# Expert products chunk by chunk for all token groups, with the down products one expert behind

## The reference

```python
logits = (x @ w_router) + b_router
top_v, top_e = lax.top_k(logits, 4)              # 4 of 32 experts per token
gates = jax.nn.softmax(top_v, axis=-1)
gu = xe @ w_gu[e] + b_gu[e]                      # xe: the rows routed to expert e, 1024 wide
gate = jnp.minimum(gu[:, :1024], 7.0)
up = jnp.clip(gu[:, 1024:], -7.0, 7.0)
act = (up + 1.0) * gate * jax.nn.sigmoid(1.702 * gate)
y = act @ w_down[e] + b_down[e]                  # weighted by the gate and added per token
```

## Time and profile before

| | us |
|---|---|
| median of 3 runs | 1584.15 |
| span of the profiled execution | 1586.3 |
| PE busy | 1548.4 (98%) |
| VectorE busy | 792.2 (50%) |
| ScalarE busy | 277.8 |
| Pool busy | 187.4 |
| gate-up products (L1333, both tiles) | 691.0 |
| down products (L1339 and L1345) | 343.3 |

### The profile page before, as it was taken

One profiled execution on the slowest core, in us unless ns is written; L12 is line 12 of the kernel. 1 busy time (PEld: TensorE's weight loads), 2 busy tenths in 40 slices (PEclk: granted clock), 3 DMA queues, 4 the chain that ended last, 5 costly groups with the idle time before them and its releaser, 6 DMA issues.

```text
span 1586.3 us, 32991 instructions
## 1 busy us (share of the span) xinstructions
PE 1548.4 (98%) x13237; PEld 717.9 (45%) x13237; DVE 792.2 (50%) x2047; ACT 277.8 (18%) x554; POOL 187.4 (12%) x269
## 2 busy tenths in 40 slices
PE   9999999999999999999999999999999999999995
PEld 7677487787745633333333333333333333333331
DVE  4349738605533645444544454445444544454448
ACT  2310020005311112111111121111111111111113
POOL 3634310014200000000000000000000000000000
PEclk9999999999999899999999999999999999999998
DMA  6555755723160599999999999999999999999995
GB/s 240 160 167 187 260 170 174 253 68 125 65 279 27 193 384 417 413 417 410 415 414 416 410 415 415 413 406 416 414 413 403 419 415 415 405 417 415 413 392 199
DMA packets 72618, 509.62 MB, mean 321 GB/s; under 512 B 13482, under 2 KB 13930, under 8 KB 47330
## 3 DMA queue, kind: packets, MB, share of 16 engines
q1 hardware_dynamic: 62298, 489.15, 77.3%
q0 software_dynamic: 10256, 19.61, 3.7%
HBM read 497.51 MB, written 19.88 MB: 326 GB/s over the span
## 4 chain that ended last, share of the span: by engine, by line
PE 70%; DMA 24%; DVE 2%; issue 1%; ACT 1%; POOL 1%; SPq 0%; DVEq 0%; POOLq 0%; ACTq 0%
PE PS L1333 33%; DMA weight_ring<-w_gu 22%; PE PS L938 16%; PE PS L1246 4%; PE PS L1339 3%; PE PS L989 2%; PE PS L1054 2%; PE PS L1345 2%; PE PS L1040 1%; PE PS L1104 1%; PE PS L1003 1%; DVE weight_ring L1844 1%; DMA y_k<-region_x,idx_y 1%; POOL weight_ring L632 1%; PE PS L1290 1%
## 5 line engine op out<-in xcount | busy, mean ns | idle before, releaser
L1333 PE MATMUL PS<-weight_ring,region_experts 128*32 128x512 f32 x5376 | 599.4, 594 | 8.5 <-DMA weight_ring<-w_gu 6.9
L1333 PEld LDWEIGHTS PS<-weight_ring,region_experts 128*32 128x32 f32 x5376 | 170.1, 110 | 404.0 <-issue 365.4
L1778 DVE TENSOR_TENSOR region_experts<-PS,region_w 128x512 f32<-128x512 f32 x96 | 66.4, 692 | 457.2 <-PE PS L1333 457.1
L1339 PE MATMUL PS<-weight_ring,act_turned 128*32 128x512 f32 x2048 | 225.6, 592 | 0.0
L938 PE MATMUL PS<-region_x,region_w 128*128 128x260 f32 (+1 forms) x928 | 209.4, 385 | 1.0 <-DVE region_x L1560 1.0
L938 PEld LDWEIGHTS PS<-region_x,region_w 128*128 128x128 f32 x928 | 175.2, 190 | 33.1 <-issue 4.6
L1769 DVE STREAM_TRANSPOSE region_experts<-region_x 32x256 f32<-32x256 f32 x372 | 161.2, 433 | 4.7
L865 ACT ACTIVATE region_experts<-region_experts 128x256 f32<-128x256 f32 x96 | 40.0, 417 | 627.4 <-DVE region_experts L1780 627.4
L1339 PEld LDWEIGHTS PS<-weight_ring,act_turned 128*32 128x32 f32 x2048 | 66.6, 110 | 153.2 <-issue 153.2
L1345 PE MATMUL PS<-weight_ring,act_turned 128*32 128x256 f32 x2048 | 117.7, 382 | 4.0 <-DVE act_turned L1790 4.0
L670 POOL DMA_INDIRECT y_k<-region_x,idx_y x32 | 30.1, 940 | 677.9 <-ACT region_x L888 580.7
(11 more groups left out here) (282 smaller groups left out, 1131.8 us busy)
## 6 DMA issues: line engine op xcount, KB each, us to landing
weight_ring<-w_gu SPq DMA_DIRECT2D x112, 2048.0 KB, 12.0
weight_ring<-w_down SPq DMA_DIRECT2D x64, 2048.0 KB, 12.4
ring_more<-w_gu SPq DMA_DIRECT2D x16, 2048.0 KB, 21.6
region_w<-w_mt SPq DMA_DIRECT2D x33, 512.0 KB, 3.9
weight_ring<-cache_kT SPq DMA_DIRECT2D x64, 256.0 KB, 4.0
weight_ring<-cache_v SPq DMA_DIRECT2D x64, 256.0 KB, 3.9
weight_ring<-w_out SPq DMA_DIRECT2D x2, 2048.0 KB, 10.1
weight_ring<-y_k SPq DMA_DIRECT2D x2, 2048.0 KB, 13.2
```

The costliest lines, as they stand in the source:

```text
L1333: mm = pe.matmul(bank(g)[GRP * q:GRP * q + GRP], hTe[u][:, k, GRP * g:GRP * g + GRP], weights(k // 2, u)[:, k % 2, SEG * q:SEG * q + SEG], ...
L1339: mm = pe.matmul(bank(3)[GRP * j:GRP * j + GRP], actT[:, kk, GRP * g:GRP * g + GRP], w_dn[:, kk, 512 * h:512 * h + 512], start=(kk == 0), ...
L1778: dve.tensor_tensor(gu, bank(g), b_wide, ALU.add).then_inc(S["biased"], 1)
```

## The change

PE now computes gate-up products chunk by chunk, all three groups within a chunk, so a chunk is given free when the third group has used it (`up`). The down products of an expert (`down`) come behind the gate-up products of the next one. There are two `actT` for that, and the down products go by halves: wide and rest products of a half together, then the half is free. The comparison and the indices are made for the expert after the next. VectorE's work of an expert is one `step`: wait for the gathered rows of the next expert and turn them, spread this expert's bias, spread the gates, `keep`, compare for the expert after the next, the three groups one after the other, and the indices of the expert after the next; Pool then gathers for these. SyncE's order per expert is chunk 0 of the next expert, the bias, chunks 1 to 3 of the next expert (`rest`), and the two down halves of this one. The last expert keeps the order by groups (`last_up`, `last_down`); the down products of expert 30 come between those of 29 and the gate-up of 31, with their first half in `W7`, loaded before chunk 0 of expert 31, and their second in slot 0, loaded behind chunk 3. The zeroing scatter of the end now stands behind the `keep` of expert 31, the rank loads go to other pieces, and VectorE adds samples and ranks behind group 2.

```diff
 SyncE
-            for c in range(2):
-                down_load(c, 0)
...
-            gu_load(0, 1, 1)
-            load(0, 1, 1, whole=False)
-            experts(0, 1)
+            def step(b, e, u):
+                n = b * NE + e
+                sp.wait_ge(S["gu_free"], (n - 1) * 3 + 1)
+                gu_load(0, e + 1, 1 - u)
+                rest(b, e)
+                for h in range(2):
+                    sp.wait_ge(S["down_done"], (n - 1) * 2 + h + 1)
+                    down_load(h, e)
+            def rest(b, e):
+                n = b * NE + e
+                sp.wait_ge(S["b_wide_done"], n + 1)
+                bias_load(e + 1)
+                for c in range(1, 3):
+                    sp.wait_ge(S["gu_free"], n * 3 + c + 1)
+                    gu_load(c, e + 1)
+                sp.wait_ge(S["round_done"], (n + 1) * ROUNDS)
+                gu_load(3, e + 1)
...
+            gu_load(0, 1, 1)
+            for h in range(2):
+                down_load(h, 0)
+            steps(0)
+            last = NE - 1
+            sp.wait_ge(S["gu_free"], (last - 2) * 3 + 1)
+            down_to(0, last - 1, W7[:, :], r_full[6])
+            sp.wait_ge(S["gu_free"], (last - 1) * 3 + 1)
+            gu_load(0, last)
+            rest(0, last - 1)
+            sp.wait_ge(S["down_done"], (last - 2) * 2 + 1)
+            down_to(1, last - 1, W6[:, slot(0):slot(1)], r_full[0])
+            sp.wait_ge(S["down_done"], (last - 2) * 2 + 2)
+            down_to(0, last, W6[:, slot(1):slot(2)], r_full[1])
+            sp.wait_ge(S["down_done"], (last - 1) * 2 + 1)
+            down_to(1, last, W7[:, :], r_full[6])
 Pool
-                    gather(b, e + 1, 1 - u)
...
+                gather(b, 0, 0)
+                gather(b, 1, 1)
+                gather(b, 2, 0)
+                gather(b, 3, 1)
+                send(b, 0, 0)
+                with po.Fori(1, NE // 2 - 1) as i:
+                    gather(b, 2 * i + 2, 0)
+                    send(b, 2 * i - 1, 1)
+                    gather(b, 2 * i + 3, 1)
+                    send(b, 2 * i, 0)
+                send(b, NE - 3, 1)
 ScalarE
+                swish(b, 0)
+                swish(b, 1)
+                y_out(b, 0, 0, 0, first)
+                with act.Fori(1, NE // 2 - 1) as i:
+                    swish(b, 2 * i)
+                    y_out(b, 2 * i - 1, 1, i - 1, first)
+                    swish(b, 2 * i + 1)
+                    y_out(b, 2 * i, 0, i, first)
 TensorE
+            def up(b, e, u, i, start=False, lead=False):
+                n = b * NE + e
+                pe.wait_ge(S["hTe_ready"], n + 1)
+                for c in range(4):
...
+                    for g in range(ROUNDS):
+                        if c == 0 and not lead:
+                            pe.wait_ge(S["biased"], (n - 1) * ROUNDS + g + 1)
+                        for k in (2 * c, 2 * c + 1):
+                            mm = gu_step(g, u, k, weights(c, u))
+                        if c == 3:
+                            mm.then_inc(S["round_done"], 1)
+                    if c < 3:
+                        mm.then_inc(S["gu_free"], 1)
+                    if lead and c == 0:
+                        turn_gates()
+                        pick_gates_first()
+            def down(n, u, at, fills):
+                pe.wait_ge(S["actT_ready"], (n + 1) * ROUNDS)
+                pe.wait_ge(S["y_ready"], n + 1)
+                for h in range(2):
+                    pe.wait_ge(r_full[at[h]], fills[h])
+                    w = half_of(at[h])
+                    for kk in range(4 * h, 4 * h + 4):
+                        mm = down_wide(u, kk, w)
+                    if h:
+                        mm.then_inc(S["wide_done"], 1)
+                    for kk in range(4 * h, 4 * h + 4):
+                        mm = down_rest(u, kk, w)
+                    mm.then_inc(S["down_done"], 1)
...
+                up(b, 0, 0, 0, start, lead=start)
+                pick(b * NE + 3, 2, 0)
+                if start:
+                    pe.wait_ge(S["gT_done"], 1)
+                up(b, 1, 1, 0, start)
+                pick(b * NE + 4, 3, 1)
+                down_in_turn(b, 0, 0, start)
+                with pe.Fori(1, NE // 2 - 1) as i:
+                    up(b, 2 * i, 0, i, start)
+                    pick(b * NE + 2 * i + 3, 2 * i + 2, 0)
+                    down_in_turn(b, 2 * i - 1, 1, start)
+                    up(b, 2 * i + 1, 1, i, start)
+                    pick(b * NE + 2 * i + 4, 2 * i + 3, 1)
+                    down_in_turn(b, 2 * i, 0, start)
+                up(b, NE - 2, 0, NE // 2 - 1, start)
+                down_in_turn(b, NE - 3, 1, start)
...
+            pick_rows_first(0)
+            keep_clock(6)
+            pick_rows_first(1)
+            keep_clock(12)
+            turn_rows_first(1)
+            steps(0, True)
...
+            down(NE - 2, 0, (6, 0), ((NE // 2) * 16, (NE - 1) * 16))
+            last_up()
+            last_down()
 VectorE
-                slot_rows(1, 0)
+                slot_rows(1, 0, bank(FIRST_AT[0], 3, 400))
+                compare(1, 1)
                 add_before(NTILE - 1)
                 choice_ranks(1, 4)
+                slot_rows(2, 1, bank(FIRST_AT[1], 3, 400))
...
+            def step(b, e, u, i, first=False, start=False, look=True, src=None):
+                n = b * NE + e
+                src = slots(u) if src is None else src
+                if start:
+                    dve.wait_ge(S["hTe_ready"], 1)
+                rows_in(b, e + 1, 1 - u, i + u)
+                widen(n)
+                if start:
+                    after_gates()
+                else:
+                    dve.wait_ge(S["y_ready"], n)
+                spread_gates(src[:, 3:6], u)
+                free_scatter(b, u, i, first)
+                keep(u, src[:, 6:7])
+                if look:
+                    compare(e + 2, u)
+                groups(b, e, u)
+                if look:
+                    slot_rows(n + 3, u, slots(u))
...
+            widen(NE - 1)
+            last_rows()
+            dve.wait_ge(S["y_ready"], NE - 1)
+            spread_gates(slots(1)[:, 3:6], 1)
+            group(NE - 1, 0, 1)
+            free_scatter(0, 1, NE // 2 - 1, True)
+            keep(1, slots(1)[:, 6:7])
+            group(NE - 1, 1, 1)
+            group(NE - 1, 2, 1)
+            add_samples(0)
+            for k in range(TOPE):
+                add_rank(k, 0)
```

More of the change, by code:

```diff
@@ L499, in experts @@
-            def experts(b, first):
-                with sp.Fori(first, NE // 2) as i:
-                    for u in range(2):
-                        load(b, i * 2 + u, u)
-            gu_load(0, 1, 1)
-            load(0, 1, 1, whole=False)
-            experts(0, 1)
+                sp.wait_ge(S["gu_free"], (n - 1) * 3 + 1)
[4 more added lines that the diff above has]
+                    down_load(h, e)
@@ L533, in _ @@
                     with sp.If(b * CAP < most):
-                        experts(b, 0)
+                        again(b)
                 ranks_load(1)
@@ new lines, in last_up @@
+            def last_up():
+                n = NE - 1
+                pe.wait_ge(S["hTe_ready"], NE)
+                for g in range(ROUNDS):
+                    pe.wait_ge(S["biased"], (n - 1) * ROUNDS + g + 1)
+                    for c in range(4):
+                        if g == 0:
+                            pe.wait_ge(r_full[2 + c], (NE // 2 + 1 if c == 0 else NE) * 16)
+                        for k in (2 * c, 2 * c + 1):
+                            mm = gu_step(g, 1, k, weights(c, 0))
+                        if g == ROUNDS - 1 and c < 3:
@@ L1771, in turn_rows, with group @@
                 ins.then_inc(S["hTe_ready"], 1)
-            def group(ne, g):
+            def group(ne, g, u):
                 gu, sg, a = gu_t[g % 2], sg_t[g % 2], act_t[g % 2]
@@ L1870, in _ @@
                         dve.wait_ge(S["slots_moved"], b)
-                        experts(b)
+                        compare(0, 0)
+                        slot_rows(b * NE + 1, 0, slots(0))
+                        compare(1, 1)
+                        slot_rows(b * NE + 2, 1, slots(1))
+                        rows_in(b, 0, 0, 0)
+                        steps(b)
+                        widen(b * NE + NE - 1)
+                        dve.wait_ge(S["y_ready"], b * NE + NE - 1)
+                        spread_gates(slots(1)[:, 3:6], 1)
+                        free_scatter(b, 1, NE // 2 - 1, False)
+                        keep(1, slots(1)[:, 6:7])
+                        groups(b, NE - 1, 1)
                 add_samples(1)
```

377 lines of the change are left out of this document (168 added, 209 removed).

## The result

The changed kernel takes **1603.26 us** (median of 4 runs, 1597.48 to 1607.06) where the kernel before takes 1584.16: the ratio is **1.0120, 95% interval 1.0099 to 1.0141**, so it is slower by 19.1 us. The forecast was 1595.7, 11.6 above the kernel before, and its range ended at 1603: the direction was right, the size was not.

The account below looks back on a forecast made before the run. The DMA weight stream was taken as the bound, 31.77 us per expert against PE's 31.28. Last gate-up start +14.1 and tail -2.5 gave +11.6 on the median 1584.15: 1595.7 us, range 1587 to 1603.

Parts of the forecast that it names:

- Start of the stream: Before the first weight load: added VectorE compare and index operations start the stream 1.2 us later, +1.2.
- The lull at 552: First expert, 552 to 560: chunk 1 of expert 1 goes out earlier, so the lull's lost 4.2 us are saved.
- The new gap: Second expert: SyncE's bias and chunk loads wait behind gather and widening, the stream runs dry, +9.5, between +6 and +12.
- The landing of the down half: End of stage: second down half of expert 30 lands at 1530.0, from the old last chunk's 1529.33 plus four terms.
- Small losses: Two dips of DMA share in each period: half of them saved, 0.2 us x 29, -5.8, between 0 and -12.5.
- The same loads must have passed when that half lands: End of stream: expert 30's second down half needs the same loads passed as the old last chunk; no extra time counted.
- The end of the stream: Expert 30's second down half lands last, with down products and a slow clock before the last gate-up, which starts +14.1.
- The tail: From the last gate-up's start to the end of the rank additions: 47.0 us becomes 44.5, -2.5, between -4.5 and +4.
- PE does not notice: Second expert's gap: chunk 1 of expert 2 lands by 590 and is used at 596, so PE loses nothing.
- Rival 1: Expert stage: the stream needs only 30.5 us per expert, PE's 31.28 rule, median 1572 to 1578 us; chance 0.27.
- Rival 2: No change: dips save 6.7 us more and the gather of expert 2 lands in 3.7 us, 1585.8 us; chance 0.16.
- Rival 3: VectorE's ring with the gather binds from a landing of 12.8 us on; 1626 us at 14 us; chance 0.07.

Follow-up runs that it names:

- i_compare_soon: Changed kernel with VectorE's compare for the fourth expert put ahead of the gather's wait, in the second expert alone: 1603.76 us, ratio 1.0119.
- b: Changed kernel with the bias widened ahead of VectorE's wait for the gathered rows: 1599.41 us, ratio 1.0097.
- c_tail_swap: Changed kernel with expert 30's second down half loaded before chunks 1 to 3 of expert 31, and chunk 0 of 31 behind them: 1598.73 us, ratio 1.0087.
- d: Changed kernel with both edits, the bias widened ahead of the rows' wait and the two last loads exchanged: 1591.89 us, ratio 1.0046.
- a0_again: The changed kernel run once more, unchanged, for more runs and a second profile: 1602.64 us, ratio 1.0117.
- h: Changed kernel with VectorE's keep of expert 31 and the scatter's release moved ahead of the last expert's first activations: 1600.48 us, ratio 1.0112.
- f_full: Changed kernel with the edits of d and h, and the last gate-up by chunks in the order 1, 2, 3, 0: 1581.27 us, ratio 0.9987.
- e_by_groups: Changed kernel with only the product order undone, gate-up products going group by group again: 1617.86 us, ratio 1.0224.
- l_both_groups: The kernel of d with gate-up products going group by group again: 1611.23 us, ratio 1.0172.
- g_direct: Changed kernel with the gather by index replaced by one plain transfer of the first 96 rows: 1622.18 us, ratio 1.0255.

## Why the prediction was right and wrong, step by step

- **What bounds the kernel.** Right for the changed kernel: i_compare_soon takes a stall out of TensorE and gains nothing, and moving loads (b, c, d) gains, in d clear of noise. In the kernel before it was read from the trace alone.
- **Start of the stream, +1.2.** 1.0 measured: the first weight load is issued at 533.68, 2.58 us after S, where 1.55 lay between before.
- **The lull at 552, -4.2.** Right as forecast: 431 GB/s where 205 were.
- **The new gap, +9.5.** Right in place and cause, 8.0 in size. Two errors on the way met by luck: VectorE's groups began before the gate-up of expert 0 had ended (550.53 against 553.8, where I let them begin behind it), and the gather then took 9.9 us to land where I took 7.
- **The landing of the down half, "1529.33 + 1.2 - 4.2 + 9.5 - 5.8 = 1530.0": this is the step that failed.** From S that is 995.3 us; measured were 995.9, and in the four other traces with the gap (a0, c, h, i) 999.1 to 1000.0. Without small losses my own terms give 994.65 + 1.0 - 4.2 + 8.0 = 999.5. So of the 5.8 us that I let the small losses save, 3.6 came in one trace and nothing, within 0.5, in four. The bytes of SyncE's queue split this into two terms, at 397 GB/s (its 356.82 MB in 900 us before):
  - *Small losses, -5.8.* I had taken half of the 12.5 us of dips of one sampled period, times 29. From 600 to 1500 the queue moved 356.82 MB before, and 358.82, 357.44, 357.56, 357.76 and 357.82 MB in these five: 5.0 us saved in the first, 1.6 to 2.5 in the others (b and d, without the gap, moved 359.08 and 358.97: 5.4 to 5.7). So the term was too large by 1 to 4 us for the kernel as it is. Rows in flight take the rate down to 326 and 344 GB/s as ever.
  - *"The same loads must have passed when that half lands."* They had not passed alone. From S to the landing the queue moved 391.30 MB before, and 392.66, 392.97, 392.90, 392.80 and 392.79 MB in these five: 1.4 to 1.7 MB more, that is 3.4 to 4.2 us, a term that I had put at nothing. The two down halves of expert 31, 4.2 MB, are issued behind the awaited half; in the chain of waits that half takes 29.04 us from issue to landing, and behind the landing (1527.05 to 1545) SyncE's queue moves only 1.88 MB more:

```profile
1497.96 29.04 DMA weight_ring<-w_down
```

```profile
q1 hardware_dynamic: 138, 1.88, 24.6%
```

  So 2.3 MB of the later loads had moved when it landed, and 0.9 MB in the kernel before (the whole is 394.54 MB). For a0_again the account closes: 5.0 us for the bytes missing up to 65 us behind S (21.04 MB for 23.01), less 1.5 for those gained in the next 900 us (357.37 for 356.77), less 2.3 for a fuller stream in the last 35, and 4.2 for the bytes that moved ahead: 5.4, which is 1000.0 - 994.65.
- **The end of the stream, "the largest term".** Right in mechanism: c_tail_swap removes it. The down half is last and TensorE waits 14.86 us ("some 17"). The rest comes at a lower clock, which costs 1.45 us in the first profile and 2.8 in a0_again, 1.7 forecast.
- **The tail, -2.5.** -1.4 in the first profile (62.1 against 63.5) and -1.2 in a0_again. The scatter is issued 12.2 us after L and lands in 3.35, as forecast with 12.7 and 3.7. The rank additions end 45.7 us after L, forecast 44.5: they wait 1.4 us for the rank rows. What follows is unchanged, 16.4 us.
- **A miss:** "PE does not notice" the gap was wrong: its pick waits 3.76 us for VectorE's compare, which stands behind the gather too. It costs nothing until the gap is repaired.
- **The periods.** Forecast were 31.3 us at first and 31.6 later; the picks stayed 31.37 apart up to the last two (31.84 and 31.62), and TensorE waited 0.2 us for chunks in 900.
- **The sum.** The profile of a0_again and that of before stand each some 4 us above their medians, so they can be compared: 1070.2 against 1051.6 from S to the end, 18.6 us, for 19.1 between the medians. 11.6 were forecast; the landing adds 4.7 (5.4 for 0.7), the clock behind it 1.0, the tail 1.3: 18.6. There is only one trace of the kernel before, and a trace can be off by 4 us, so each of these sizes is good to some microseconds and no better.
- **Rival 1** (TensorE bound, faster) needed a stream under 31.2 us for an expert. The slow stretches stayed, against it; but with the start and the end of the stream repaired, f_full is nearly this case: TensorE without a DMA wait up to the end. L came at S + 983.1, within the rival's 978 to 984, and 63.0 us stood behind it, where the rival had 61.0. **Rival 2** fell with the gap. **Rival 3**, VectorE's ring, needed gathers that land in 12.8 us or more; from 600 to 1500 they landed in 9.8 to 11.2, and VectorE had 2.7 us of slack per expert, as the prediction had it.

The Trainium skill (DMA: Bandwidth & Descriptors, Specifications) gives 435 GB/s as the ceiling of a core's fabric. The trace agrees: the changed kernel holds 431 GB/s over the 10 us shown above and 415 over 900 us, below that figure by more where rows are in flight (378 at 562 to 570, beside a gather).

What the forecast lacked altogether is that the change has a strong half. With the down products put behind, product order by chunks is worth 15 to 20 us (e_by_groups, l_both_groups), and without it the rest would cost twice as much. I had counted of it only the lull (-4.2) and a part of the small losses.

## What to carry to other kernels

Ask of a load queue not only how many bytes but which instruction lets each load go: a small load (8 KB of bias) behind a wait that has nothing to do with it emptied a full stream for 8 us. Moving one line ahead of another closed that gap, and then look again: the next wait in the same queue opened a smaller one, and 3.2 us of time were gained. At the end of a stream, order the last loads by use and count the work that stands behind the last one; here that was 6.6 to 8 us in the traces, 3.9 in the medians. Don't let a load land by the bytes ahead of it alone: loads queued behind it moved 2.3 MB before it was complete. And do not multiply a dip of one period by the number of periods: sum the queue's bytes over the whole stage and compare those.

## What the runs showed of the hardware beyond what I expected

The time lost after an idle stretch of TensorE is not told by its length. The granted clock in the changed kernel (stretches, third last column):

```profile
1518.00:1520.00 2.00, 0.00 (x0) 0.00 (x0) 0.00 (x0) 0.00 (x0) 0.00 (x0) 0.50 0.98 418
...
1528.00:1530.00 2.00, 2.00 (x16) 0.49 (x12) 0.00 (x0) 0.00 (x0) 0.00 (x0) 0.51 0.71 303
1530.00:1532.00 2.00, 2.00 (x24) 0.54 (x20) 0.00 (x0) 0.00 (x0) 0.00 (x0) 1.00 0.56 238
```

It fell to the lower level (0.50, 1.2 GHz) while TensorE stood still and came back about 3 us after work began. After waits of 14.86 and 17.32 us the next products took 5.07 and 5.02 us for 3.62, 1.4 lost. But after 14.83 us in a0_again they took 6.40, after 11.74 us 6.55 and after 6.86 us 23.42 for 20.77: 2.65 to 2.9 lost, with the clock low for 5 to 6 us. A wait of only 2.06 us before the first down half of expert 30 cost 1.7 us in seven of the thirteen traces of changed kernels (5.34 for 3.64) and nothing in the six others. So a single trace may hold such a loss or not, and it should be read before two spans are compared.

With 3.4 MB more of rows SyncE's queue moved 9.5 MB less (g_direct). The same scatter landed in 3.35 us on an idle DMA and in 12.38 beside the last weights. And a deeper queue makes each load wait longer: the down halves issued from 1440 on landed 12.4 to 13.5 us after their issue before, and 24.5 to 29.7 us in the changed kernel, at nearly the same rate.
